# Second block's attention: two heads' values stationary on the halves of TensorE's array, exponentials divided before their turn, and no turn of the output

## The chip, the cores and the metric

The kernel runs on one NeuronCore of a Trainium2 chip, as one program in one launch. The metric is the device time of one execution in microseconds. Five engines run their own instruction streams in order and meet only at semaphores: TensorE (PE), which multiplies and turns (transposes), VectorE (DVE), ScalarE (ACT), GpSimd (POOL), and SyncE (SP), which here only starts the loads of the weights.

## The reference

Two transformer blocks in float32 on 256 tokens of width 1024. The first has differential attention, retention and a feed-forward part that picks among 16384 experts. The second has a state-space mixer (SSD, 16 heads of 64), a latent attention (MLA, 16 heads), a memory attention and a convolved feed-forward part. The change is in the latent attention of the second block, which for each of 16 heads computes

```python
scores = (q_h @ k_h.T) * 96 ** -0.5        # 256 x 256, q and k of width 96 (64 + 32 rotated)
p = softmax(where(causal by blocks of 64, scores, -inf))
out[:, h * 64:(h + 1) * 64] = p @ v_h      # values of width 64
```

The 1024 columns of `out` and the 1024 of the SSD mixer are then multiplied with a weight matrix of 2048 x 1024 and added to the residual stream.

## The kernel before

Tokens lie in two tiles of 128 (`t` = 0, 1). Most products are in a form that adds three products of rounded parts (a high and a low part of each operand), so weights stream in through SP, ACT rounds the high part of each slot (`hi_parts`, line L1580), POOL subtracts for the low part (L523), and PE multiplies. PE gives each slot back through the semaphore `spent`. The small products of attention are in plain float32. The trace shows each of those as two passes (a matmul of the program has two rows on PE), and a turn as one.

The attention of the second block and the convolution of the SSD mixer are written as one loop over the heads `h` = 0 to 15, once for each engine, with the order written out by hand. I call one turn of this loop an iteration. In iteration `h`

- PE makes the scores of head `h + 2` (`mla_scores`, L1241), turns the exponentials of head `h` into bank 5 (`mla_turn`, L1251), turns queries or keys (`qk_turn`, L1231), multiplies one slot of the SSD input, `xbc(7 + h)` up to `h` = 8 (L565, L566, L570), then `z_late` (L574, L575, L579) up to `h` = 12, then `out_half`, the first slots of the output matrix (same lines). In some iterations there are small products (`cb_product`, L1214; `cum`, L1203) and turns of the SSD input (`xs_turn`, L1222). Last comes `mla_out(h)` (L1261): exponentials times values.
- DVE masks the scores of `h + 2` and takes their maximum (`masked`, L2979, L2982), copies the turned exponentials of `h` to SBUF (L3044), convolves SSD channels (`conv(6 + h)`, L2901 to L2907, five instructions) and does the mask of `cb` (L2998, L2999) and `xs_out` (L3007, L3008).
- ACT copies turned queries and keys (`qk_out`, L2022, L2024), makes the exponentials of head `h + 2` and their sums (`mla_exp`, L2035), and rounds one weight slot (L1580). In iterations 2, 6 and 10 it applies Silu to four convolved tiles (`xbc_silu`, L1991), which takes a load of its function table, and one back for the exponential.

`xbc(pos)` writes one of two PSUM banks, so PE waits there until `conv(pos - 2)` is done: `if pos >= 4: pe.wait_ge(s["conv_done"], 4 * (pos - 1))`. In iteration `h` that is the convolution that DVE does in its iteration `h - 1`.

The output of head `h` comes out with tokens on the partitions, undivided, in bank 6, four heads at a time. Then DVE divides four heads by their sums (`divided`, L2989, L2990) into `o_m`, PE turns it (`out_turn`, L1271, in iterations 6 and 10 and after the loop), ACT makes the high part (`out_hi`, L2043) and DVE the low part (`out_lo`, L3014) of `m_t`, which `out_half` multiplies with the output matrix. After the loop comes the loop over the 16 SSD heads, in which PE waits for each head on a chain PE (`seg_sum`, L1277), DVE (`clip`, L3028), ACT (`seg_exp`, L2080, L2081), DVE (`weigh`, L3021), and does `out_half` in every second head.

Of the kernel before, what the change touches and what calls it, by code (L numbers as in the profile page):

```python
# [30 lines left out]
P = 128  # L31
# [167 lines left out]
OUT_AT = {6: (0, 3), 10: (1, 0)}  # L199
# [59 lines left out]
def _places(parts):  # L259
# [25 lines left out]
    kcat=(13312, 16384), seg=(14336, 16384), v_m=(16384, 18432), q_t=(18432, 22528), m_hi=(18432, 20480), m_lo=(20480, 22528),  # L285
    k_t=(22528, 26624), lat_hi=(22528, 23808), lat_lo=(23808, 25088), row_t=(25088, 25344), o_m=(27648, 29696), dts=(29696, 30208),
# [7 lines left out]
def two_blocks(nc, weights, consts, cols_in, rows_in, x_in, mem_in, pos_in, out):  # L294
    with ExitStack() as ctx:
# [61 lines left out]
        def row(name):  # L357
# [32 lines left out]
        o_m = area("o_m", "p (t c) -> p t c", t=TT)  # L390
# [28 lines left out]
            "cum_copied", "up_first", "xs_turned", "xdt_made", "o_turned", "group_factor", "mla_masked",  # L419
            "seg_sum", "seg_clipped", "seg_exp", "seg_weighed", "ssd_out",  # L420
            "group_root", "trig_arg", "trig_done", "kv_rotated",
            "mla_scores", "mla_shift", "mla_exp", "mla_turned", "mla_t_copied", "mla_out", "mla_out_copied",
# [130 lines left out]
        def _(pe):  # L553
# [691 lines left out]
            def mla_turn(h):  # L1245

                pe.wait_ge(s["mla_exp"], h + 1)
                if h:
                    pe.wait_ge(s["mla_t_copied"], h)
                for k in range(3):  # L1250
                    mm = pe.transpose(bank[:, 5, k * P:(k + 1) * P], e_m[:, h % 2, k * P:(k + 1) * P], ident)  # L1251
                mm.then_inc(s["mla_turned"], 1)

            def mla_out(h):

                pe.wait_ge(s["mla_t_copied"], h + 1)
                if h % 4 == 0 and h:
                    pe.wait_ge(s["mla_out_copied"], h // 4)
                for t in range(TT):
                    for k in range(t + 1):  # L1260
                        mm = pe.matmul(bank[:, 6, t * T + h % 4 * 64:t * T + h % 4 * 64 + 64], et_m[:, h % 2, t + k, :],  # L1261
                                       v_m[:, k, h * 64:(h + 1) * 64], start=(k == 0), stop=(k == t))
                mm.then_inc(s["mla_out"], 1)

            def out_turn(pair, to):

                pe.wait_ge(s["mla_out_copied"], pair + 1)
                for b in (2 * pair, 2 * pair + 1):
                    for t in range(TT):
                        at = (b % 2) * T + t * P  # L1270
                        mm = pe.transpose(bank[:, to, at:at + P], o_m[:, t, b * P:(b + 1) * P], ident)  # L1271
                mm.then_inc(s["o_turned"], 1)
# [38 lines left out]
            for h in range(MH):  # L1311
# [46 lines left out]
                mla_out(h)  # L1358
# [3 lines left out]
            out_turn(2, 7)  # L1362
            out_half(0, 1, m_t)
            done = AHEAD
            for h in range(SH):
# [8 lines left out]
                if h == 0:  # L1374
                    pe.wait_ge(s["mla_out_copied"], 4)
                if h == 4:
# [10 lines left out]
                if h == 0:  # L1387
                    low("mla_out", 5)
                    out_turn(3, 7)
# [176 lines left out]
        def _(act):  # L1566
# [473 lines left out]
            def out_hi(pair, at):  # L2040
                act.wait_ge(s["o_turned"], pair + 1)
                for b in (2 * pair, 2 * pair + 1):
                    nc.scalar.copy(m_t[0][:, b, :], bank[:, at, (b % 2) * T:(b % 2 + 1) * T]).then_inc(s["split_act"], 1)  # L2043
# [11 lines left out]
            hi_parts(M + 3)  # L2055
            for h in range(MH):
                for i in QK_AT.get(h, ())[:1]:
                    qk_out(i, 7)
                if h + 2 < MH:
# [3 lines left out]
                if h == 10:  # L2063
                    out_hi(*OUT_AT[h])
# [4 lines left out]
                if h == 6:  # L2069
                    out_hi(*OUT_AT[h])  # L2070
# [14 lines left out]
            out_hi(2, 7)  # L2085
# [13 lines left out]
            for h in range(SH):  # L2099
                if h:  # L2100
                    seg_exp(h)
                if h == 2:
                    out_hi(3, 7)
# [164 lines left out]
        def _(dve):  # L2268
# [717 lines left out]
            def divided(i):  # L2986
# [353 lines left out]
```

## Time and profile before

| what | value |
|---|---|
| median of 3 runs | 1451.14 us (1450.7 to 1451.85) |
| profiled execution, time | 1453.91 us |
| profiled execution, span on the core | 1452.1 us |
| PE busy | 1434.8 us, 99% of the span |
| DVE, ACT, POOL busy | 949.9, 825.6, 890.9 us |
| the chain that ended last | PE 90% |
| granted clock of TensorE, mean | 0.999 |
| the loop over the 16 heads, from PE's first scores in it to the first SSD head | 1060.7 to 1142.3 us of the span |

The span is what the profiler saw on the core; the time is that of the same execution by the device's clock and is 1.8 us longer. The profiled execution took 2.8 us more than the median.

### The profile page before, as it was taken

What the parts mean: (1) busy time and instruction counts of PE and PEld (TensorE: products, weight loads), DVE (VectorE), ACT (ScalarE), POOL (GpSimd) and SP (SyncE); (2) the same over time, 40 slices, a digit from 0 to 9 for tenths busy, and PEclk for the clock granted to TensorE, in tenths of its full rate; (3) what the DMA queues carried; (4) which work ended last, traced back from release to release, by engine and by line L of the source; (5) the groups of instructions that cost most, each with busy time, mean ns of one, the idle gap of its engine ahead of it and who ended that gap; (6) DMA issues with size and microseconds to landing.
All of it is one profiled execution on the core that took longest, in us unless ns stands there. A gap on an engine that the chain in (4) does not pass through costs nothing.

```text
span 1452.1 us, 25628 instructions
## 1 busy us (share of the span) xinstructions
PE 1434.8 (99%) x8868; PEld 1284.9 (88%) x8868; DVE 949.9 (65%) x2022; ACT 825.6 (57%) x1481; POOL 890.9 (61%) x711
## 2 busy tenths in 40 slices
PE   8999999999999999999999999999999999999997
PEld 6788999999999999888888888888899889888886
DVE  4664399948889999665555555334687633387776
ACT  6576555456666665554454554447666766644454
POOL 6749898987777777200000003997944576599986
PEclk9999999999999999999999999999999999999999
DMA  7535667655555555555555555655643454466664
GB/s 255 161 102 182 180 189 233 196 181 151 162 157 159 161 165 162 183 193 197 189 194 198 188 195 191 190 182 183 194 129 91 160 153 138 136 190 193 191 189 130
DMA packets 137590, 253.09 MB, mean 174 GB/s; under 512 B 16464, under 2 KB 18896, under 8 KB 136848
## 3 DMA queue, kind: packets, MB, share of 16 engines
q1 hardware_dynamic: 135392, 243.79, 53.7%
q10 hardware_dynamic: 1872, 6.41, 1.3%
q8 instruction: 63, 1.03, 0.3%
q0 software_dynamic: 224, 1.54, 0.3%
q14 instruction: 39, 0.32, 0.1%
HBM read 248.54 MB, written 3.15 MB: 173 GB/s over the span
## 4 chain that ended last, share of the span: by engine, by line
PE 90%; POOL 4%; DVE 2%; issue 2%; ACT 2%; DMA 1%; SPq 0%; POOLq 0%; ACTq 0%; DVEq 0%
PE bank L556 13%; PE bank L558 13%; PE bank L557 13%; PE bank L574 5%; PE bank L579 5%; PE bank L1517 5%; PE bank L575 5%; PE bank L570 5%; PE bank L565 5%; PE bank L566 5%; POOL w_both L523 3%; PE bank L1520 3%; PE bank L1002 2%; PE bank L1029 2%; PE bank L1032 1%
## 5 line engine op out<-in xcount | busy, mean ns | idle before, releaser
L523 POOL TENSOR_TENSOR w_both<-ring,w_both 128x512 fp32r<-128x512 f32 x688 | 873.4, 1299 | 546.2 <-ACT w_both L1580 537.7
L1580 ACT CAST w_both<-ring 128x1024 fp32r<-128x1024 f32 x452 | 474.7, 1051 | 378.8 <-PE bank L558 176.3
L2773 DVE TENSOR_TENSOR w_both<-ring,w_both 128x1024 fp32r<-128x1024 f32 x111 | 136.0, 1225 | 124.6 <-ACT w_both L1580 123.3
L556 PE MATMUL bank<-w_both,act_hi 128*128 128x512 f32 x512 | 199.5, 390 | 0.4 <-DVE act_lo L2778 0.4
L557 PE MATMUL bank<-w_both,act_hi 128*128 128x512 f32 x512 | 199.4, 389 | 0.0
L558 PE MATMUL bank<-w_both,act_lo 128*128 128x512 f32 x512 | 199.2, 389 | 0.0
L557 PE MATMUL bank<-h_both,w_both 128*128 128x256 f32 x648 | 183.4, 283 | 0.0
L556 PE MATMUL bank<-h_both,w_both 128*128 128x256 f32 x648 | 183.3, 283 | 0.0
L558 PE MATMUL bank<-h_both,w_both 128*128 128x256 f32 x648 | 183.3, 283 | 0.0
L565 PE MATMUL bank<-h_both,w_both 128*128 128x256 f32 x568 | 141.6, 287 | 0.0
L566 PE MATMUL bank<-h_both,w_both 128*128 128x256 f32 x568 | 139.2, 283 | 0.0
L556 PEld LDWEIGHTS bank<-h_both,w_both 128*128 128x128 f32 x648 | 124.4, 192 | 0.0
L558 PEld LDWEIGHTS bank<-h_both,w_both 128*128 128x128 f32 x648 | 124.4, 192 | 0.0
L557 PEld LDWEIGHTS bank<-h_both,w_both 128*128 128x128 f32 x648 | 124.3, 192 | 0.0
L556 PEld LDWEIGHTS bank<-w_both,act_hi 128*128 128x128 f32 x512 | 96.2, 188 | 20.5 <-DVE w_both L2773 0.8
L558 PEld LDWEIGHTS bank<-w_both,act_lo 128*128 128x128 f32 x512 | 96.1, 188 | 20.1
L557 PEld LDWEIGHTS bank<-w_both,act_hi 128*128 128x128 f32 x512 | 96.2, 188 | 19.4
L566 PEld LDWEIGHTS bank<-h_both,w_both 128*128 128x128 f32 x568 | 108.9, 192 | 0.2
L565 PEld LDWEIGHTS bank<-h_both,w_both 128*128 128x128 f32 x568 | 108.8, 191 | 0.2
L2726 DVE TENSOR_TENSOR hots<-bank,chosen_t 128x1024 fp32r<-128x1024 f32 x64 | 78.4, 1224 | 10.1 <-PE bank L1002 6.0
L570 PE MATMUL bank<-h_both,w_both 128*128 128x256 f32 x600 | 83.9, 283 | 0.0
L574 PE MATMUL bank<-w_both,h_both 128*128 128x512 f32 (+2 forms) x208 | 81.8, 395 | 0.4 <-issue 0.3
(482 smaller groups left out, 2711.0 us busy)
## 6 DMA issues: line engine op xcount, KB each, us to landing
ring<-weights_in SPq DMA_DIRECT2D x910, 256.0 KB, 3.0
mem_kv<-arena ACTq DMA_DIRECT2D x2, 1024.0 KB, 6.9
arena<-mem_kv ACTq DMA_DIRECT2D x2, 1024.0 KB, 8.4
ring<-weights_in SPq DMA_DIRECT2D x8, 200.0 KB, 2.6
ring<-weights_in SPq DMA_DIRECT2D x8, 144.0 KB, 2.4
xres<-x_in SPq DMA_DIRECT2D x2, 512.0 KB, 5.3
arena<-mem_in POOLq DMA_DIRECT2D x1, 1024.0 KB, 8.5
arena<-rows_in ACTq DMA_DIRECT2D x2, 512.0 KB, 4.1
```

The lines of the kernel that those rows point to most:

```text
L523: nc.gpsimd.tensor_tensor(w_lo[:, k, at], ring[:, k, at], w_hi[:, k, at].bitcast(F32), ALU.subtract).then_inc(s[done], 1)
L556: pe.matmul(out_, a[0], b[0], start=start, stop=False, **kw)
L557: pe.matmul(out_, a[0], b[1], start=False, stop=False, **kw)
L558: return pe.matmul(out_, a[1], b[0], start=False, stop=stop, **kw)
L565: pe.matmul(out_, w[0], b[0], start=start, stop=False, skip_group_check=True)
L566: return pe.matmul(out_, w[0], b[1], start=False, stop=False, skip_group_check=True)
L570: return pe.matmul(out_, w[1], b[0], start=False, stop=stop, skip_group_check=True)
L574: pe.matmul(out_, x[0], w[0], start=start, stop=False, skip_group_check=True)
L575: return pe.matmul(out_, x[1], w[0], start=False, stop=False, skip_group_check=True)
L1580: nc.scalar.copy(w_hi[:, k, :], ring[:, k, :]).then_inc(s["hi_made"], 1)
L2726: link(v.tensor_tensor(hots, iota8, chosen_t[:, 0:2, 4 * g:4 * g + 4].unsqueeze(3).broadcast_to([P, 2, 4, NK]), ALU.is_equal))
L2773: v.tensor_tensor(w_lo[:, k, :], ring[:, k, :], w_hi[:, k, :].bitcast(F32), ALU.subtract)\
```

## The change

`mla_out` takes two heads at once, at the end of odd iterations only. The values of a head (128 keys by 64) are now the stationary operand and lie in one half of the array's columns, the two heads in the two halves; the turned exponentials are the moving operand, 256 tokens for the first 128 keys and 128 tokens for the second. The output has channels on the partitions and tokens along the row, which is what `m_t` needs, so `o_m`, `divided` and `out_turn` are gone. Since the tokens are then no longer on the partitions, the exponentials are divided before they are turned: DVE takes the reciprocal of the sums of one head (`inverse`), and ACT scales the exponentials in place (`e_scaled`). PE's turn waits for that instead of for the exponential. `out_hi` and `out_lo` take 256 columns of bank 6 after each pair of heads, in even iterations, and `mla_out` of the next pair waits for `out_lo`. `m_lo` moves to where `o_m` was.

```diff
             def mla_turn(h):
-                pe.wait_ge(s["mla_exp"], h + 1)
+                pe.wait_ge(s["mla_scaled"], h + 1)
...
-            def mla_out(h):
-
-                pe.wait_ge(s["mla_t_copied"], h + 1)
-                if h % 4 == 0 and h:
-                    pe.wait_ge(s["mla_out_copied"], h // 4)
-                for t in range(TT):
-                    for k in range(t + 1):
-                        mm = pe.matmul(bank[:, 6, t * T + h % 4 * 64:t * T + h % 4 * 64 + 64], et_m[:, h % 2, t + k, :],
-                                       v_m[:, k, h * 64:(h + 1) * 64], start=(k == 0), stop=(k == t))
+            def mla_out(pair):
+
+                pe.wait_ge(s["mla_t_copied"], 2 * pair + 2)
+                if pair:
+                    low("mla_out", pair - 1)
+                for k in range(TT):
+                    for e in range(2):
+                        h = 2 * pair + e
+                        mm = pe.matmul(bank[64 * e:64 * e + 64, 6, k * P:T], v_m[:, k, h * 64:(h + 1) * 64],
+                                       et_m[:, e, 2 * k:2 + k, :].rearrange("p k q -> p (k q)"), start=(k == 0), stop=(k == 1),
+                                       skip_group_check=True)
                 mm.then_inc(s["mla_out"], 1)
-
-            def out_turn(pair, to):
...
-                if h == 10:
-                    pe.wait_ge(s["conv_done"], 60)
-                    out_turn(1, 0)
...
-                    out_turn(0, 3)
...
-                mla_out(h)
+                if h % 2:
+                    mla_out(h // 2)
...
+            def e_scaled(h):
+                act.wait_ge(s["mla_inverse"], h + 1)
+                for t in range(TT):
+                    e = e_m[:, h % 2, t * P:t * P + (t + 1) * P]
+                    ins = nc.scalar.mul(e, e, dts[:, 256 + t * MH + h:257 + t * MH + h])
+                ins.then_inc(s["mla_scaled"], 1)
+
+            def out_hi(pair):
+                act.wait_ge(s["mla_out"], pair + 1)
+                nc.scalar.copy(m_t[0][:, pair, :], bank[:, 6, 0:T]).then_inc(s["split_act"], 1)
...
             hi_parts(M + 3)
+            e_scaled(0)
             for h in range(MH):
                 for i in QK_AT.get(h, ())[:1]:
                     qk_out(i, 7)
+                if h + 1 < MH:
+                    e_scaled(h + 1)
                 if h + 2 < MH:
                     mla_exp(h + 2)
                 if h in (2, 6, 10):
                     xbc_silu(h + 2)
-                if h == 10:
-                    out_hi(*OUT_AT[h])
+                if h % 2 == 0 and h:
+                    out_hi(h // 2 - 1)
                 if 3 + h < 16:
                     hi_parts(M + 4 + h)
...
+            def inverse(h):
+                dve.wait_ge(s["mla_exp"], h + 1)
+                v.reciprocal(m_div[:, :, h:h + 1], m_sum[:, :, h:h + 1]).then_inc(s["mla_inverse"], 1)
...
+            def out_lo(pair):
+                dve.wait_ge(s["split_act"], SPLIT["mla_out"] + pair + 1)
+                v.tensor_tensor(m_t[1][:, pair, :], bank[:, 6, 0:T], m_t[0][:, pair, :].bitcast(F32), ALU.subtract).then_inc(s["lo_made"], 1)
...
             for h in range(MH):
+                if h + 1 < MH:
+                    inverse(h + 1)
                 if h + 2 < MH:
                     masked(h + 2)
-                if h % 4 == 0 and h:
-                    divided(h // 4 - 1)
                 dve.wait_ge(s["mla_turned"], h + 1)
                 if h >= 2:
-                    dve.wait_ge(s["mla_out"], h - 1)
+                    dve.wait_ge(s["mla_out"], h // 2)
                 v.tensor_copy(et_m[:, h % 2, :, :], bank[:, 5, 0:3 * P].rearrange("p (k q) -> p k q", q=P))\
                     .then_inc(s["mla_t_copied"], 1)
-                if h - 1 in OUT_AT:
-                    out_lo(*OUT_AT[h - 1])
+                if h % 2 == 0 and h:
+                    out_lo(h // 2 - 1)
                 if 6 + h < 16:
                     conv(6 + h)
```

After the loop `out_hi(7)` stands behind `seg_exp(0)` on ACT and `out_lo(7)` between `weigh(0)` and `clip(1)` on DVE, where `out_hi(2)`, `divided(3)` and `out_lo(2)` stood. `out_turn(2)` and `out_turn(3)` with their parts are gone.

**ACT, iteration 6 of the loop.** In the kernel before these are the exponentials of head 8 (L2035), the table load and the four Silu (L1991), the weight slot (L1580), and the two high parts of the turned output (L2043):

```order
L2024 ACTIVATE arena<-bank 96x512 [waits qk_turned]
L2022 COPY arena<-bank 96x512 [waits qk_turned]
L2035 ACTIVATE work,arena<-bank,arena 128x128 [waits mla_turned,mla_shift]
L2035 ACTIVATE work,arena<-bank,arena 128x256
L1991 ACT_TABLE_LOAD
L1991 ACTIVATE arena<-arena 128x256 [waits conv_done] x4
L1580 CAST w_both<-ring 128x1024 [waits spent,slot_loaded_1]
L2043 CAST m_hi<-bank 128x256 [waits o_turned]
L2043 CAST m_hi<-bank 128x256
```

In the changed kernel L2026 is `e_scaled(7)`, L2017 the exponentials of head 8, L1973 Silu, L2031 `out_hi(2)` and L1562 the weight slot:

```order
L2006 ACTIVATE arena<-bank 96x512 [waits qk_turned]
L2004 COPY arena<-bank 96x512 [waits qk_turned]
L2026 ACTIVATE work<-work,arena 128x128 [waits mla_inverse]
L2026 ACTIVATE work<-work,arena 128x256
L2017 ACTIVATE work,arena<-bank,arena 128x128 [waits mla_turned,mla_shift]
L2017 ACTIVATE work,arena<-bank,arena 128x256
L1973 ACT_TABLE_LOAD
L1973 ACTIVATE arena<-arena 128x256 [waits conv_done] x4
L2031 CAST m_hi<-bank 128x256 [waits mla_out]
L1562 CAST w_both<-ring 128x1024 [waits spent,slot_loaded_1]
```

Two scalings came in ahead of the exponentials, and the high part moved from behind the weight slot to right behind the Silu. Iteration 2 has the same order now and had no high part before.

**DVE, iteration 6 of the loop, and on to iteration 7.** Before, the copy of the turned exponentials (L3044) was followed by `conv(12)` and then by the masking of the next iteration:

```order
L2982 TENSOR_REDUCE arena<-bank 128x1
L3044 COPY work<-bank 128x384 [waits mla_out,mla_turned]
L2901 TENSOR_TENSOR bank<-bank,arena 128x256 [waits spent]
L2903 TENSOR_SCALAR arena<-bank,cols 128x256 [waits xbc_scaled]
L2907 SCALAR_TENSOR_TENSOR arena<-bank,cols,arena 128x255 [waits conv_done]
L2907 SCALAR_TENSOR_TENSOR arena<-bank,cols,arena 128x254 [waits conv_done]
L2907 SCALAR_TENSOR_TENSOR arena<-bank,cols,arena 128x253 [waits conv_done]
L2979 TENSOR_TENSOR bank<-bank,arena 128x2x128 [waits mla_exp,mla_scores]
```

Now L3025 is the copy, L2995 `out_lo(2)`, which waits through `split_act` for `out_hi(2)`, and L2888 the first instruction of `conv(12)`; L2975 is `inverse(8)`:

```order
L2969 TENSOR_REDUCE arena<-bank 128x1
L3025 COPY work<-bank 128x384 [waits mla_out,mla_turned]
L2995 TENSOR_TENSOR m_lo<-bank,m_hi 128x256 [waits split_act]
L2888 TENSOR_TENSOR bank<-bank,arena 128x256 [waits spent]
L2890 TENSOR_SCALAR arena<-bank,cols 128x256 [waits xbc_scaled]
L2894 SCALAR_TENSOR_TENSOR arena<-bank,cols,arena 128x255 [waits conv_done]
L2894 SCALAR_TENSOR_TENSOR arena<-bank,cols,arena 128x254 [waits conv_done]
L2894 SCALAR_TENSOR_TENSOR arena<-bank,cols,arena 128x253 [waits conv_done]
L2975 RECIPROCAL arena<-arena 128x2 [waits mla_exp]
```

The low part of a pair of heads came in between the copy and the convolution, in every even iteration from 2 on.

**PE, end of iteration 5.** Before, the last rows of the iteration and the first of the next (L1214 is `cb_product`, L1261 `mla_out(5)`, L1241 the scores of head 8, L1251 the turn of head 6):

```order
L1214 MATMUL bank<-arena 128x256
L1261 MATMUL bank<-arena,work 128x64 [waits mla_t_copied]
L1261 MATMUL bank<-arena,work 128x64 x2
L1241 MATMUL bank<-arena 128x128 [waits mla_exp,qk_out_act]
L1241 MATMUL bank<-arena 128x256
L1251 MATMUL bank<-cst,work 128x128 [waits mla_t_copied,mla_exp]
```

Now (L1212, L1260 for heads 4 and 5, L1239, L1249):

```order
L1212 MATMUL bank<-arena 128x256
L1260 MATMUL bank<-work,arena 64x256 [waits lo_made,mla_t_copied]
L1260 MATMUL bank<-work,arena 64x256
L1260 MATMUL bank<-work,arena 64x128 x2
L1239 MATMUL bank<-arena 128x128 [waits mla_exp,qk_out_act]
L1239 MATMUL bank<-arena 128x256
L1249 MATMUL bank<-cst,work 128x128 [waits mla_t_copied,mla_scaled]
```

Three narrow products per head became four wider ones per pair of heads, each on 64 output partitions, with a wait for the low part of the pair before, and the turn waits for the scaled exponentials.

## Rows read from the trace of the kernel before

**Rows 1.** The page, busy time, share of the span, instructions.
```profile
PE 1434.8 (99%) x8868; PEld 1284.9 (88%) x8868; DVE 949.9 (65%) x2022; ACT 825.6 (57%) x1481; POOL 890.9 (61%) x711
```

**Rows 2.** Groups by line, 1050 to 1190 us: busy us, mean ns.
```profile
L1261 PE MATMUL bank<-arena,work 128*128 128x64 f32 x96 | 12.5, 267 | 0.0
...
L3014 DVE TENSOR_TENSOR m_lo<-bank,m_hi 128x256 fp32r<-128x256 f32 x8 | 3.0, 417 | 0.0
...
L2122 ACT ACTIVATE arena<-arena 128x256 f32<-128x256 f32 x4 | 1.7, 498 | 0.3 <-DVE arena L3102 0.3
...
L2989 DVE RECIPROCAL arena<-arena 128x8 f32<-128x8 f32 x4 | 0.8, 195 | 0.0
```

**Rows 3.** Timeline of PE in and behind the loop: start us, length us.
```profile
1061.39 0.49 PE L1251 MATMUL bank<-cst,work 128*128 128x128 f32 x3
...
1073.04 0.87 PE L1241 MATMUL bank<-arena 96*128 96x128 f32 x4
...
1080.27 0.36 PE L565 MATMUL bank<-h_both,w_both 128*128 128x256 f32 x1
...
1096.81 0.87 PE L1241 MATMUL bank<-arena 96*128 96x128 f32 x4
...
1101.16 0.60 PE L1271 MATMUL bank<-cst,arena 128*128 128x128 f32 x4
1101.59 0.78 PE L1261 MATMUL bank<-arena,work 128*128 128x64 f32 x6
1102.21 0.87 PE L1241 MATMUL bank<-arena 96*128 96x128 f32 x4
...
1103.61 0.36 PE L565 MATMUL bank<-h_both,w_both 128*128 128x256 f32 x1
...
1115.03 0.50 PE L574 MATMUL bank<-w_both,h_both 128*128 128x512 f32 x1
...
1123.64 0.63 PE L1222 MATMUL bank<-cst,arena 128*128 128x128 f32 x4
```

**Rows 4.** Timeline of ACT, before the loop and in iteration 6.
```profile
1060.99 1.05 ACT L1580 CAST w_both<-ring 128x1024 fp32r<-128x1024 f32 x1 [0.48 <-PE bank L570]
...
1098.49 0.58 ACT L2022 COPY arena<-bank 96x512 f32<-96x512 f32 x1 [1.80 <-PE bank L1231]
1098.97 0.36 ACT L2035 ACTIVATE work<-bank,arena 128x128 f32<-128x128 f32 x1
...
1099.90 1.28 ACT L1991 ACT_TABLE_LOAD   x1
1101.19 1.34 ACT L1991 ACTIVATE arena<-arena 128x256 f32<-128x256 f32 x4
1102.43 1.03 ACT L1580 CAST w_both<-ring 128x1024 fp32r<-128x1024 f32 x1
```

**Rows 5.** Timeline of DVE in iterations 6 and 8.
```profile
1099.19 0.42 DVE L2901 TENSOR_TENSOR bank<-bank,arena 128x256 f32<-128x256 f32 x1
...
1100.23 1.52 DVE L2907 SCALAR_TENSOR_TENSOR arena<-bank,cols,arena 128x255 f32<-128x255 f32 x3
...
1114.29 0.68 DVE L3008 TENSOR_TENSOR arena<-bank,arena 128x512 f32<-128x512 f32 x1
```

**Rows 6.** Timeline of PE: products on row halves, and on the whole array.
```profile
90.77 1.13 PE L847 MATMUL bank<-arena 64*128 64x256 f32 x8
91.84 0.50 PE L574 MATMUL bank<-w_both,h_both 128*128 128x512 f32 x1
...
1089.06 1.03 PE L1214 MATMUL bank<-arena 128*128 128x256 f32 x4
1089.93 0.78 PE L1261 MATMUL bank<-arena,work 128*128 128x64 f32 x6
```

**Rows 7.** Stretches at the end: us, PE busy (x), granted clock, DMA share, GB/s.
```profile
1446.00:1448.00 2.00, 0.00 (x0) 1.00 0.00 0
1448.00:1450.00 2.00, 0.00 (x0) 0.69 0.87 312
```

More of the change, by code:

```diff
@@ L418, in two_blocks @@
             "xbc_silu", "latent_summed", "rotated", "y_ready", "y_summed", "y_scaled", "y_scaled_late", "qk_turned", "qk_out_act",
[L419 removed]
+            "cum_copied", "up_first", "xs_turned", "xdt_made", "group_factor", "mla_masked",
             "seg_sum", "seg_clipped", "seg_exp", "seg_weighed", "ssd_out",
             "group_root", "trig_arg", "trig_done", "kv_rotated",
[L422 removed]
+            "mla_scores", "mla_shift", "mla_exp", "mla_turned", "mla_t_copied", "mla_out", "mla_inverse", "mla_scaled",
             "mem_scores", "mem_shift", "mem_exp", "mem_scaled", "mem_turned", "mem_t_copied", "mem_out", "mem_out_copied",
@@ L1386, in _ @@
                           start=False, stop=True).then_inc(s["ssd_out"], 1)
-                if h == 0:
-                    low("mla_out", 5)
-                    out_turn(3, 7)
             while done < 2 * KD:
@@ L2038, in mla_exp @@
                 ins.then_inc(s["mla_exp"], 1)
[L2040 to L2043, printed above, removed]
+            def e_scaled(h):
[7 more added lines that the diff above has]
+                nc.scalar.copy(m_t[0][:, pair, :], bank[:, 6, 0:T]).then_inc(s["split_act"], 1)
             act.dma_start(area("mask"), consts[:, CAT["mask"][0]:CAT["mask"][1]]).then_inc(s["mask_loaded"], 16)
@@ L2084, in _ @@
             seg_exp(0)
-            out_hi(2, 7)
+            out_hi(7)
             def y_squares(g):
@@ L2984, in masked @@
                 ins.then_inc(s["mla_shift"], 1)
-            def divided(i):
-                dve.wait_ge(s["mla_out"], 4 * i + 4)
-                hs = slice(4 * i, 4 * i + 4)
-                link(v.reciprocal(m_div[:, :, hs], m_sum[:, :, hs]))
-                v.tensor_tensor(o_m[:, :, i * T:(i + 1) * T].rearrange("p t (h c) -> p t h c", c=64),
-                                bank[:, 6, :].rearrange("p (t h c) -> p t h c", t=TT, c=64),
-                                m_div[:, :, hs].unsqueeze(3).broadcast_to([P, TT, 4, 64]), ALU.mult)\
-                    .then_inc(s["mla_out_copied"], 1)
+            def inverse(h):
+                dve.wait_ge(s["mla_exp"], h + 1)
+                v.reciprocal(m_div[:, :, h:h + 1], m_sum[:, :, h:h + 1]).then_inc(s["mla_inverse"], 1)
             def cb_mask(g):
@@ L3009, in xs_out @@
                     .then_inc(s["xdt_made"], 1)
-            def out_lo(pair, at):
-                dve.wait_ge(s["split_act"], SPLIT["mla_out"] + 2 * pair + 2)
-                for b in (2 * pair, 2 * pair + 1):
-                    v.tensor_tensor(m_t[1][:, b, :], bank[:, at, (b % 2) * T:(b % 2 + 1) * T], m_t[0][:, b, :].bitcast(F32), ALU.subtract)\
-                        .then_inc(s["lo_made"], 1)
+            def out_lo(pair):
+                dve.wait_ge(s["split_act"], SPLIT["mla_out"] + pair + 1)
+                v.tensor_tensor(m_t[1][:, pair, :], bank[:, 6, 0:T], m_t[0][:, pair, :].bitcast(F32), ALU.subtract).then_inc(s["lo_made"], 1)
             def weigh(h):
@@ L3033, in _ @@
             masked(1)
+            inverse(0)
             conv(5)
@@ L3079, in _ @@
             weigh(0)
-            divided(3)
+            out_lo(7)
             clip(1)
-            out_lo(2, 7)
             dve.wait_ge(s["copied_act"], COPY["z_late"][0] + 2)
@@ L3088, in _ @@
                 weigh(h + 1)
-                if h == 2:
-                    out_lo(3, 7)
                 if h in (4, 8, 12):
```

19 lines of the change are left out of this document (2 added, 17 removed).

## The prediction

> **What bounds the kernel now.** I read the page first: PE is busy for 1434.8 us of the span of 1452.1, DVE for 65% of it [rows 1]. So PE's own work is the time, and a change is worth what it takes off PE less what it makes PE wait. Then I read the timelines of PE, ACT and DVE over the loop, to see how close behind PE the others are. I name times by their distance from an iteration's start on PE. In iteration 6 (start 1096.81) PE reaches the next slot of the SSD input, `xbc(14)`, at 1103.61, that is at 6.8 [rows 3]. It needs `conv(12)` there, whose five instructions DVE runs from 1099.19 to 1101.75 (1100.23 + 1.52), so they end at 4.95 [rows 5]. The slack is 1.85 us. It is the number on which this prediction turns.
>
> **Work taken off PE.** `mla_out` of a head holds PE for 0.62 us (1101.59 to 1102.21 [rows 3]; 96 passes in all, six per head [rows 2]). Sixteen of them make 9.8 us. A turn of the output holds it for 0.43 (1101.16 to 1101.59 [rows 3]) with four transposes; the other three stand in a denser place, so I take 0.37 for them, and 1.5 for all four.
>
> **Work put on PE.** Each pair has four products, that is eight passes: four over 256 columns, four over 128. On the whole array four passes over 256 columns take 0.87 us (1089.06 to 1089.93), 0.215 each. One after the other the pair would take 4 x 0.215 + 4 x 0.108 = 1.29 us. No row shows column halves, but the retention's products on row halves alternate in the same way: eight passes over 256 columns from 90.77 to 91.84, 1.07 us where the whole array would need 1.72 [rows 6]. That is just five lengths: a product's second pass runs beside the first pass of the product on the other half, and only the first and the last are alone. The same count for the new pair gives 1 + 1 + 0.5 + 0.5 + 0.5 + 0.5 = 4 lengths, 0.86 us. Going to halves and back costs something, since the first weight loads cannot be early; the bounds are 0.86 and 1.07 (the row itself), and I take 0.95. Eight pairs make 7.6 us. Net of work: 7.6 - 9.8 - 1.5 = -3.7 us.
>
> The Trainium skill speaks against this price. "TensorEngine Tiling (Array Packing)", Key Properties, says that a change of tiling mode drains the engine; a row that shows the drain alone is not there, and by that rule the pair would be nearer 1.07. "TensorE: Matmul & The Clock Gate", Part 3 (The mechanism), says that a weight load overlaps with a running product only when the row groups differ, and two column halves share all rows. By that rule little of the overlap is left; it is the rival of no overlap below.
>
> **The wait at the start.** On ACT `e_scaled(0)` stands behind a weight slot that runs from 1060.99 to 1062.04 [rows 4], because the slot's place comes free only when PE has finished the slot before the loop. PE turned head 0 at 1061.39 [rows 3]. The price of two scalings in place (128 and 256 columns) has no row. Nearest is a scaling of 256 columns in place, 0.50 us [rows 2]; below it lies the 0.36 of an exponential of 128 [rows 4]. For the two, pipelined, the bounds are 0.65 and 1.0; I take 0.75. So PE turns head 0 at 1062.75: a wait of 1.35 us.
>
> **The waits in iterations 3 and 7.** Take iteration 6. ACT copies the turned queries at 1.68 and starts the exponentials at 2.16, the table load at 3.09, Silu at 4.38 to 5.72 [rows 4]. Now `e_scaled(7)` comes before the exponentials: Silu ends at 6.45. Behind it stands `out_hi(2)`, about 0.35 us: 6.8. On DVE `out_lo(2)` stands between the copy and `conv(12)` and waits for that, then takes 0.42 [rows 2]: 7.2. What is queued behind it is the whole convolution, 2.56 us: it ends at 9.8 instead of 4.95. PE comes to `xbc(14)` at 6.8 less the turn of 0.43 and the `mla_out` of 0.62 that left iteration 6, so at 5.75. It waits **4.0 us**. Iteration 2 has the same chain. There PE came to `xbc(10)` at 80.27 - 73.04 = 7.2 [rows 3], now 0.6 earlier, 6.6, and `conv(8)` ends at 9.7: a wait of **3.0 us**. In iterations 4, 8 and 12 there is no Silu, so `out_hi` ends at 4.2 and the convolution at 7.1, which PE meets with hardly a wait. In iteration 8, however, the convolution is followed by `xs_out(1)`, whose end at 1114.97 [rows 5] lies right ahead of the part of `z_late` that needs its bank, at 1115.03 [rows 3]: no slack. `out_lo(3)` with its wait and the reciprocal put it 1.0 us later on balance (the division of four heads is gone from DVE), and PE comes 0.6 us earlier: 1.6 us.
>
> **The wait in iteration 11.** PE's `xs_turn` at 1123.64 [rows 3] already follows the last Silu of iteration 10. That Silu starts with the scores of iteration 10 and not with PE's later work, so the `mla_out` and the turn that left iteration 10 (1.0 us) only bring PE there earlier, and DVE's reciprocal adds 0.15: 1.15 us more. Behind the loop `e_scaled(15)`, two high parts and a low part stand ahead of the first SSD heads on ACT and DVE, while a turn is gone from PE: an estimate of 0.8 us with what is left over in iterations 5 and 13, between 0 and 1.5.
>
> **The sum.** Waits 1.35 + 3.0 + 4.0 + 1.6 + 1.15 + 0.8 = 11.9 us, work -3.7: +8.2 us. The rest is free: the scalings of the other heads lie in idle time of ACT (it waits 1.80 us in iteration 6 [rows 4]), the weight slots are rounded three slots ahead, and the division that leaves DVE was hidden. Nothing later gives the loss back, because PE is the bound on both sides of the loop. The profiled execution would go from 1453.9 to 1462.1; on the median, 2.8 lower, 1451.1 becomes **1459.4 us**.
>
> **Rivals.**
> 1. *The work counts and the convolution does not wait.* Then -3.7 is nearly all: 1447.4. For it: ACT and DVE are far from full [rows 1]. Against it: both rows of order are hard, and a load of ACT's table and Silu (2.6 us) lie between. It decides at waits of 3.7 us in all; the one of iteration 7 alone passes that. With about half of my waits the result is no change.
> 2. *The column halves do not overlap.* The pair takes 1.29 plus 0.1; eight cost 3.5 us more, a little of it inside waits: 1462.5. For it: no row has column halves. Against it: the row halves count out to five lengths exactly.
> 3. *The clock falls in a wait.* Behind the last matmul the granted clock still is 1.00 from 1446 to 1448 with PE idle, and 0.69 in the next stretch [rows 7], so it fell from 2.4 to 1.2 GHz near 1448.8, when PE had been idle for more than 2.8 us. Waits of 3.0 and 4.0 us are in that region. Work from 1096.81 to 1101.16 [rows 3], 4.35 us, would take twice that at the lower level; with one fall, part of it hidden by the next wait, 3 us more: 1462.5.
>
> **How the numbers follow.** My forecast 0.6, rival 2 0.14, rival 3 0.12, rival 1 0.06, half the waits (near no change) 0.08. The forecast's own range: scalings -0.3 to +0.8, pairs -0.7 to +1.0, the last term -0.8 to +0.7, so 1457.6 to 1461.9. Rivals 2 and 3 with their errors reach to 1466; below, 1454.5 leaves rival 1 and no change outside. Within 0.2% (2.9 us) is what a measurement of this kernel can't tell from no change. Faster 0.06, same 0.08, slower 0.86.
>
> **What the new profile would show.** Two waits of PE on DVE's convolution, 3.0 us before `xbc(10)` and 4.0 before `xbc(14)`; ahead of each, DVE idle with ACT's high part as the releaser. A wait of 1.35 us of PE on ACT's scaling at the loop's start. Eight groups of eight passes of about 0.95 us each, instead of sixteen of 0.62. The loop up to the first SSD head 8 us longer than the 81.6 before, with the same time on both sides of it. I am wrong if the low part finds its high part ready in iterations 2 and 6, or if a group takes 1.3 us, or if the clock is below 1.00 in the loop.

## The result, and the profile after

The changed kernel takes 1462.38 us (median of 6 runs, 1461.15 to 1462.74), the kernel before 1451.22 (6 runs, 1450.62 to 1452.54). The ratio is 1.0073, with a 95% interval of 1.0063 to 1.0083: 11 us slower, where 8.2 were predicted. The time lies 3.0 us above the forecast. That is 0.5 us outside the forecast's own range (1457.6 to 1461.9), but inside the wider one (1454.5 to 1466) that counts rivals 2 and 3 in, and both of these had put it at 1462.5. So the time alone doesn't tell which of them came; the rows and the experiments do.

The page of the changed kernel, busy time, share of the span and instructions, answers to [rows 1]:

```profile
PE 1433.8 (98%) x8820; PEld 1279.0 (88%) x8820; DVE 945.7 (65%) x2030; ACT 836.7 (57%) x1513; POOL 892.2 (61%) x711
```

PE is busy for 1.0 us less and the span is 1460.5 us, 8.4 more: on balance the loss is idle time of PE. (The busy time holds the slow stretches shown below, so it fell by less than the work did.) The view of waits of PE on others, from 1040 to 1200 us (us in total, times, longest), names the places; in the kernel before it has one row there, of 0.2 us and ahead of the loop:

```profile
PE bank L563 <- DVE arena L2894: 6.6, 2, 3.7
PE bank L572 <- DVE arena L2990: 1.3, 1, 1.3
PE bank L1249 <- ACT work L2026: 1.2, 1, 1.2
PE bank L1220 <- ACT arena L1973: 0.9, 1, 0.9
PE bank L1268 <- DVE arena L3001: 0.4, 1, 0.4
```

L563 is `xbc`, which waits for the convolution (L2894); L572 `z_late`, which waits for `xs_out` (L2990); L1249 the turn of head 0 behind its scaling (L2026); L1220 `xs_turn` behind Silu (L1973); L1268 the sums of an SSD head. These are the places of the forecast. The releasers can be followed in the timelines (start us, length us, in brackets the idle time before and who ended it). PE, answering to [rows 3]:

```profile
1078.22 0.60 PE L1229 MATMUL bank<-cst,arena 128*96 128x128 f32 x4
1081.67 0.38 PE L563 MATMUL bank<-h_both,w_both 128*128 128x256 f32 x1 [2.85 <-DVE arena L2894]
...
1086.00 0.74 PE L1229 MATMUL bank<-cst,arena 128*96 128x128 f32 x4
...
1105.08 0.60 PE L1229 MATMUL bank<-cst,arena 128*96 128x128 f32 x4
1109.39 0.39 PE L563 MATMUL bank<-h_both,w_both 128*128 128x256 f32 x1 [3.71 <-DVE arena L2894]
...
1113.85 0.60 PE L1220 MATMUL bank<-cst,arena 128*128 128x128 f32 x4
```

ACT in iteration 6, answering to [rows 4]:

```profile
1101.90 0.81 ACT L2026 ACTIVATE work<-work,arena 128x128 f32<-128x128 f32 x2
...
1103.52 1.28 ACT L1973 ACT_TABLE_LOAD   x1
1104.82 1.33 ACT L1973 ACTIVATE arena<-arena 128x256 f32<-128x256 f32 x4
1106.06 0.35 ACT L2031 CAST m_hi<-bank 128x256 fp32r<-128x256 f32 x1
```

DVE in iteration 6, answering to [rows 5]:

```profile
1101.66 0.55 DVE L3025 COPY work<-bank 128x384 f32<-128x384 f32 x1
1106.44 0.42 DVE L2995 TENSOR_TENSOR m_lo<-bank,m_hi 128x256 fp32r<-128x256 f32 x1 [4.23 <-ACT m_hi L2031]
1106.78 0.42 DVE L2888 TENSOR_TENSOR bank<-bank,arena 128x256 f32<-128x256 f32 x1
...
1107.82 1.51 DVE L2894 SCALAR_TENSOR_TENSOR arena<-bank,cols,arena 128x255 f32<-128x255 f32 x3
```

This is the predicted chain: DVE stands still for 4.23 us at the low part of a pair of heads until ACT, behind the table load and four Silu, has made the high part; the convolution queued behind it ends at 1109.3, and PE begins `xbc(14)` at 1109.39. It could have begun at 1105.44 (a turn takes 0.36 before the next slot starts, as everywhere in the loop), so the wait is 3.95 us. In iteration 2 the same rows stand at 1078.72 to 1081.6, and `xbc(10)` starts 3.1 us late. (The idle time in brackets is smaller, because it is counted from the modelled end of the last matmul.)

The groups by line, from 1050 to 1190 us (busy us, mean ns of one, idle time before), answer to [rows 2]:

```profile
L2026 ACT ACTIVATE work<-work,arena 128x256 f32<-128x256 f32 x16 | 7.9, 496 | 0.0
L2026 ACT ACTIVATE work<-work,arena 128x128 f32<-128x128 f32 x16 | 6.4, 401 | 7.4 <-DVE arena L2975 7.4
L1260 PE MATMUL bank<-work,arena 128*64 128x256 f32 x32 | 5.2, 404 | 0.0
...
L2995 DVE TENSOR_TENSOR m_lo<-bank,m_hi 128x256 fp32r<-128x256 f32 x8 | 3.4, 422 | 15.8 <-ACT m_hi L2031 15.8
L1260 PE MATMUL bank<-work,arena 128*64 128x128 f32 x32 | 3.1, 273 | 0.0
```

The eight low parts take 3.4 us and wait 15.8 for their high parts. Most of that does not reach PE; the two waits of 4.23 us do.

The stretches of 2 us around the two waits (PE busy and its instructions, granted clock, share of the DMA engines, GB/s) answer to [rows 7] and show what the forecast left out of its sum:

```profile
1078.00:1080.00 2.00, 0.82 (x8) 1.00 0.00 0
1080.00:1082.00 2.00, 0.33 (x2) 1.00 0.01 3
1082.00:1084.00 2.00, 2.00 (x15) 0.72 0.70 220
1084.00:1086.00 2.00, 2.00 (x11) 0.50 0.11 39
1086.00:1088.00 2.00, 2.00 (x16) 0.93 0.00 0
1106.00:1108.00 2.00, 0.00 (x0) 1.00 0.00 0
1108.00:1110.00 2.00, 0.61 (x5) 1.00 0.10 12
1110.00:1112.00 2.00, 2.00 (x13) 0.55 0.68 239
1112.00:1114.00 2.00, 2.00 (x13) 0.60 0.03 11
1114.00:1116.00 2.00, 2.00 (x18) 1.00 0.00 0
```

Behind each of the two waits the clock fell to its lower level, 1.2 GHz. The slot `xbc(10)` takes 4.33 us (1081.67 to 1086.00) and `xbc(14)` 4.46 (1109.39 to 1113.85), where a slot of the same form at 1.00 takes 2.95 (1073.42 to 1076.37): 1.4 and 1.5 us more. The turn behind `xbc(10)` takes 0.68 us where it takes 0.53 at 1.00, another 0.15. These are the costs in this one execution; in other profiled executions with the same waits a fall costs up to 2.8 us (see the kernels `heads_in_turn` and `first_scaling_early`).

The loop from the first scores to the first SSD head takes 91.5 us instead of 81.6, that is +9.9. What is behind it takes 0.5 more. Ahead of the loop, where both kernels run the same program, the profiled execution of the kernel before was 2.1 us longer than that of the changed one. Its first scores for the loop start at 1056.54, in the changed kernel at 1054.45, and in the ten experiments below between 1053.4 and 1055.2, so it is the profile of before that stands apart. Of the 2.1 us, 0.7 is in waits of PE for rounded weights and other parts from 990 us on (0.9 against 0.2); the rest isn't attributed. That accounts for most of why the profiles differ by 8.4 us and the medians by 11.2; some 0.7 us between the two stays open.

### The profile page after: what moved, and what is told of

The parts are those of the page before. It is cut to its first block, busy times and chain, and to the rows that moved or that the text cites. A ratio compares the mean times of both kernels' runs of the same rounds, so it can differ in the third digit from the quotient of the medians.

```text
span 1460.5 us, 25572 instructions
## 1 busy us (share of the span) xinstructions
PE 1433.8 (98%) x8820; PEld 1279.0 (88%) x8820; DVE 945.7 (65%) x2030; ACT 836.7 (57%) x1513; POOL 892.2 (61%) x711
## 4 chain that ended last, share of the span: by engine, by line
PE 88%; DVE 4%; ACT 3%; POOL 2%; issue 2%; DMA 1%; SPq 0%; ACTq 0%; POOLq 0%; DVEq 0%
PE bank L554 13%; PE bank L556 13%; PE bank L555 13%; PE bank L1499 5%; PE bank L568 5%; PE bank L577 5%; PE bank L572 5%; PE bank L573 5%; PE bank L563 5%; PE bank L564 5%; PE bank L1502 3%; PE bank L1000 2%; POOL w_both L521 2%; PE bank L1027 2%; PE bank L1030 1%
## 5 line engine op out<-in xcount | busy, mean ns | idle before, releaser
L1562 ACT CAST w_both<-ring 128x1024 fp32r<-128x1024 f32 x452 | 474.2, 1050 | 375.3 <-PE bank L556 175.4
L563 PE MATMUL bank<-h_both,w_both 128*128 128x256 f32 x568 | 142.9, 289 | 6.6 <-DVE arena L2894 6.6
L563 PEld LDWEIGHTS bank<-h_both,w_both 128*128 128x128 f32 x568 | 109.7, 193 | 7.3 <-DVE arena L2894 7.1
L572 PE MATMUL bank<-w_both,h_both 128*128 128x512 f32 (+2 forms) x208 | 81.8, 395 | 1.7 <-DVE arena L2990 1.3
```

The lines of the kernel that those rows point to most:

```text
L563: pe.matmul(out_, w[0], b[0], start=start, stop=False, skip_group_check=True)
L572: pe.matmul(out_, x[0], w[0], start=start, stop=False, skip_group_check=True)
L1562: nc.scalar.copy(w_hi[:, k, :], ring[:, k, :]).then_inc(s["hi_made"], 1)
```

## The experiments

Each kernel is the changed one with the edit shown. Times are medians; the kernel before, measured beside each, is given with it. The last four add up edits.

**VectorE's low part behind the convolution** (`low_after_conv`). It tells whether the order on DVE makes the two long waits.

```diff
-                if h % 2 == 0 and h:
-                    out_lo(h // 2 - 1)
                 if 6 + h < 16:
                     conv(6 + h)
+                if h % 2 == 0 and h:
+                    out_lo(h // 2 - 1)
```

> The changed kernel with one edit: on DVE the low part of a pair stands behind the convolution of its iteration instead of ahead of it. Theory (the order makes the convolution late): the waits of PE before xbc(10) and xbc(14), 3.1 and 3.95 us, vanish, and with them the two stretches at the lower clock (2.9 us); the wait of iteration 9 stays at 1.5 to 1.8 us, since the low part still stands ahead of xs_out. Time 1452.5 us. Rival (the added scalings and reciprocals load ACT and DVE, wherever they stand): the waits shrink little and the time stays above 1459. Rival (the products on column halves are dear): no change, 1462.

Measured: 1452.81 us against 1452.27, ratio 1.0002 (0.9992 to 1.0011). PE's wait for L2894 is gone, the mean clock goes from 0.997 to 0.998, and 0.0071 of the time, 10.3 us, is back. The two waits (7.05 us) and the two falls of the clock (2.9 us) come to 9.95. One place in an order carries nearly the whole loss.

**ScalarE's high part ahead of the table load and Silu** (`high_before_silu`). The same chain, cut at its other end: DVE's order stays.

```diff
-                if h in (2, 6, 10):
-                    xbc_silu(h + 2)
                 if h % 2 == 0 and h:
                     out_hi(h // 2 - 1)
+                if h in (2, 6, 10):
+                    xbc_silu(h + 2)
```

> The changed kernel with one edit: on ACT the high part of a pair stands ahead of the table load and the four Silu of iterations 2, 6 and 10 instead of behind them. Theory: the high part ends 4.2 us behind the iteration's start and the convolution 7.1 behind it, so PE waits 0.5 us before xbc(10) and 1.4 before xbc(14) in place of 3.1 and 3.95; the clock stays at full level. Time 1454.5 us. Rival (load of ACT and DVE, not order): above 1459.

Measured: 1454.81 us against 1452.27, ratio 1.0018 (1.0009 to 1.0028). Two waits for the convolution stay (0.20 and 1.06 us of idle time, before `xbc(10)` and `xbc(14)`), since the low part still waits for the high part, which ACT makes behind scalings and exponentials. The mean clock is 0.999.

**PE kept at work in the two long waits** (`filler`). It takes the clock's fall out of the loss and leaves the waits: 15 and 23 products whose result nothing reads, in iterations 3 and 7, ahead of the slot that has to wait.

```diff
+                if h in (3, 7):
+                    pe.wait_ge(s["mla_exp"], h + 2)
+                    for i in range(15 if h == 3 else 23):
+                        pe.matmul(bank[:, 4, T:2 * T], h_t[0][:, 0, 0:P], h_t[0][:, 0, 0:T], start=True, stop=True, skip_group_check=True)
```

> The changed kernel with idle time filled: in iterations 3 and 7 PE runs 15 and 23 more products (128x256 of rounded parts, 0.12 us each, result unused) in front of the slot that it waits for. They fit into the waits of 3.1 and 3.95 us, so nothing starts later. Theory (the clock fell because PE was idle for so long, and that cost 2.9 us by itself): the granted clock stays at 1.00 through the loop and the time is 1459.5 us. Rival (the fall has another cause, or the slow stretches would have been waited for anyway): 1462.4 us.

Measured: 1460.04 us against 1452.27, ratio 1.0054 (1.0038 to 1.0071). The stretches around the second wait, of this kernel, in the same columns:

```profile
1106.00:1108.00 2.00, 1.41 (x12) 1.00 0.00 0
1108.00:1110.00 2.00, 1.63 (x13) 1.00 0.43 125
1110.00:1112.00 2.00, 2.00 (x19) 1.00 0.48 137
```

The clock stays at 1.00, and the first slot takes 2.98 us (1082.12 to 1085.10) instead of 4.33. The convolution still comes as late as it did. The gain is 0.0019 of the time, 2.8 us, between the ratios' medians; the intervals of the two overlap, so its size rests on the rows more than on the times. Against the next kernel, which was measured beside this one and has the changed kernel's waits, it is 2.4 us (1462.45). PE is not busy all through: 1.07 us of idle time stay ahead of `xbc(10)`, and no fall follows.

**The products of a pair, head by head** (`heads_in_turn`). The forecast counted "five lengths" for a group on halves, because a product's second pass was taken to run beside the first pass of the next product, in the program's order. With the order changed so that both products of one head come first, that count gives more.

```diff
-                for k in range(TT):
-                    for e in range(2):
+                for e in range(2):
+                    for k in range(TT):
```

> The changed kernel with the four products of a pair in the order head, then keys, so that both products of one head stand together instead of alternating between the column halves. Theory (passes run in order, and only passes on different halves overlap): 5.5 lengths of a pass over 256 columns instead of 4, the group goes from 0.80 to about 1.12 us, eight groups give 2.6 us: 1465.0 us. Rival (the halves do not overlap, the passes are cheap for another reason): group and time as in the changed kernel, 0.80 and 1462.4.

Measured: 1462.45 us against 1452.27, ratio 1.0068 (1.0051 to 1.0085), and a group of 0.81 us. The order makes no difference, so the count by order fell.

The profiled execution of this kernel (1463.88 us, above its median) shows something else. The clock falls here while PE is still idle, and the slot starts at the lower level. The stretches up to `xbc(14)`, which starts at 1109.65:

```profile
1107.65:1108.65 1.00, 0.00 (x0) 1.00 0.00 0
1108.65:1109.65 1.00, 0.00 (x0) 0.64 0.00 0
```

The slot then takes 5.29 us instead of 4.46, and the turn behind it 0.93 instead of 0.53: this fall costs 2.7 us, with the same wait ahead of it (3.71 us of idle time in both).

**Both heads on the same half of the columns** (`same_half`). The second head's product goes to other columns of the bank, which nothing reads, so the output leaves out the odd heads.

```diff
-                        mm = pe.matmul(bank[64 * e:64 * e + 64, 6, k * P:T], v_m[:, k, h * 64:(h + 1) * 64],
+                        mm = pe.matmul(bank[0:64, 6, e * T + k * P:(e + 1) * T], v_m[:, k, h * 64:(h + 1) * 64],
```

> The changed kernel with both heads of a pair on the same half of the array's columns, in two places of the PSUM bank; the output of the second head of each pair is then not used, and output is wrong in those channels. Theory (the two halves run abreast, each with its own stream, in whatever order the products stand): here the eight passes run one after the other, 4 x 0.215 + 4 x 0.108 = 1.29 us and about 0.15 for the start and end, the group goes from 0.80 to about 1.4 us and the time up by 8 x 0.6 = 4.8 us: ratio to before 1.011. Rival (64 columns of weights make a pass cheap by themselves): 0.80 and no change.

Measured: 1467.63 us against 1452.21, ratio 1.0105 (1.009 to 1.0121), and a group of 1.44 us. The time holds more of the clock's fall than the changed kernel's profile does (the slot `xbc(14)` takes 5.29 us here), so the comparison rests on the groups. They stand so in the timelines of PE: the changed kernel, with the instruction behind it,

```profile
1071.18 0.87 PE L1260 MATMUL bank<-work,arena 128*64 128x256 f32 x8
1071.98 0.92 PE L1239 MATMUL bank<-arena 96*128 96x128 f32 x4
```

and the kernel with one half:

```profile
1071.58 1.51 PE L1260 MATMUL bank<-work,arena 128*64 128x256 f32 x8
1073.02 0.92 PE L1239 MATMUL bank<-arena 96*128 96x128 f32 x4
```

How many passes run at once can be read from stretches of L1260 alone, some 0.2 us long (the count in brackets is of the passes under way in the stretch). With one half of the columns:

```profile
1071.50:1071.75 0.25, 0.17 (x1) 1.00 0.00 0
1071.75:1072.00 0.25, 0.25 (x2) 1.00 0.00 0
```

With both halves, head by head (a pass begun in one stretch still counts in the next):

```profile
1071.55:1071.80 0.25, 0.17 (x2) 1.00 0.00 0
1071.80:1072.00 0.20, 0.20 (x4) 1.00 0.00 0
```

On one half a second pass joins only after the first stretch; on two halves two are there from the beginning, though in the program three more passes of head 0 stand ahead of the first of head 1. So the two halves work off their products independently. The trace does not name the head of a record; that the second is of the other head follows from the kernel with one half, where it isn't there.

**The first scaling ahead of the weight slot** (`first_scaling_early`).

```diff
+            e_scaled(0)
             hi_parts(M + 3)
-            e_scaled(0)
```

> The changed kernel with one edit: on ACT the scaling of head 0 stands ahead of the weight slot before the loop instead of behind it. Theory (the wait at the loop's start comes from that slot, which can begin only when PE has finished the slot before the loop): the wait of 1.4 us goes and nothing else changes, 1461.0 us. Rival (the scaling itself is late because the reciprocal is): 1462.4.

Measured: 1461.62 us against 1452.21, ratio 1.0065 (1.005 to 1.008). The wait at L1249 is gone from PE's waits; the gain of 0.0008, 1.2 us, is inside the intervals. In the profiled execution the clock falls during both long waits again, and `xbc(14)` takes 5.28 us.

**Both orders mended** (`both_moves`): the first scaling early, and the low part at the end of DVE's iteration.

```diff
+            e_scaled(0)
             hi_parts(M + 3)
-            e_scaled(0)
...
-                if h % 2 == 0 and h:
-                    out_lo(h // 2 - 1)
                 if 6 + h < 16:
                     conv(6 + h)
...
+                if h % 2 == 0 and h:
+                    out_lo(h // 2 - 1)
```

> The changed kernel with the first scaling ahead of the weight slot and the low part of a pair at the end of its DVE iteration, behind the convolution and xs_out. Theory: the waits at the start (1.4 us), of the convolution (7.0), of iteration 9 (1.3) and the clock's 2.9 us go; 1.3 us stay in iteration 11 and at the first SSD heads. Ratio to before 0.9988 (1.7 us faster). Rival (each removed wait comes back at the next place): not faster than before.

Measured: 1451.54 us against 1452.21, ratio 0.9994 (0.9985 to 1.0004). PE's waits from 1050 to 1200 us:

```profile
PE bank L1220 <- ACT arena L1973: 1.2, 1, 1.2
PE bank L572 <- DVE arena L2990: 0.7, 1, 0.7
PE bank L1268 <- DVE arena L3001: 0.4, 1, 0.4
PE bank L1229 <- ACT arena L2006: 0.4, 1, 0.4
```

**Four moves** (`four_moves`): besides, in iteration 10 ACT's Silu goes ahead of the exponentials, and the last low part behind `clip(1)`.

```diff
+                if h == 10:
+                    xbc_silu(h + 2)
                 if h + 2 < MH:
                     mla_exp(h + 2)
-                if h in (2, 6, 10):
+                if h in (2, 6):
                     xbc_silu(h + 2)
...
-            out_lo(7)
             clip(1)
+            out_lo(7)
```

> The kernel both_moves with two more moves: in iteration 10 the Silu stands ahead of the exponentials on ACT, and behind the loop the last low part stands behind the second clip on DVE. Theory: the waits of iteration 11 (0.9 us) and of the first SSD heads (0.4) go as well; ratio to before 0.998 (3.0 us faster), which is the work that left PE less what its switches cost. Rival (the table load for the exponential now comes late for the heads 12 and 13): as both_moves or slower.

Measured: 1450.9 us against 1452.21, ratio 0.9991 (0.9982 to 1.0). The waits at L1220 and L1268 are gone, and a new one came: PE waits 1.0 us at `mla_out(5)` for the copy of turned exponentials. The timeline of DVE shows what made that copy late:

```profile
1122.56 0.43 DVE L2997 TENSOR_TENSOR m_lo<-bank,m_hi 128x256 fp32r<-128x256 f32 x1 [4.55 <-ACT m_hi L2031]
...
1123.96 0.55 DVE L3027 COPY work<-bank 128x384 f32<-128x384 f32 x1
```

The low part waits for its high part in `both_moves` too, 3.42 us. With the Silu brought forward, the table load back and the exponentials stand ahead of the high part as well, so it comes 1.0 us later (1122.16 instead of 1121.14), and so does the copy behind the low part.

**The high part first on ScalarE, with two moves and with four** (`high_first`, `five_moves`). The edit of both:

```diff
+                if h % 2 == 0 and h:
+                    out_hi(h // 2 - 1)
                 if h + 1 < MH:
                     e_scaled(h + 1)
...
-                if h % 2 == 0 and h:
-                    out_hi(h // 2 - 1)
```

> The version with both moves (first scaling early, VectorE's low half of the output at the end of its iteration), and in the even iterations of ScalarE the rounded high half of the output comes first, ahead of the scaling of exponentials. Theory (what is left of the loss is in single waits of the even iterations, and ScalarE's order sets them): the low half never waits for the high half; the wait of 0.7 us for the low half (L572) and that of 0.4 us for the scaling shrink by together some 0.6 us or the second grows to 0.8, the waits of 1.2 us at the Silu (L1220) and 0.4 us at the first SSD head stay. Ratio to before about 0.999 (1450.8 us), against 0.9994 of the version without the move. Rival: the scaling, now 0.35 us later, is late for its values product in every even iteration, and the ratio rises to 1.001.

> The version with four moves, and the high half of the output first on ScalarE in the even iterations. Theory: in iteration 10 the low half's wait of 4.55 us for the high half goes, and with it the 1.0 us that TensorE waited for the copy of the fifth pair's sums (L1260 on L3027); ratio to before about 0.998 (1449.3 us) where the version with four moves has 0.9991. Rival: the wait comes back at the next place in the row, as it did with four moves, and the ratio stays at 0.999.

Measured: with two moves 1449.82 us, ratio 0.9987 (0.9978 to 0.9996); with four 1449.5 us, ratio 0.9986 (0.9977 to 0.9995), against 1451.73. The waits of PE in the same stretch, with two moves,

```profile
PE bank L1220 <- ACT arena L1973: 1.0, 1, 1.0
PE bank L1268 <- DVE arena L3001: 0.8, 2, 0.4
PE bank L1229 <- ACT arena L2006: 0.4, 1, 0.4
```

and with four:

```profile
PE bank L1260 <- DVE work L3027: 0.4, 1, 0.4
PE bank L1229 <- ACT arena L2006: 0.4, 1, 0.4
PE bank L1268 <- DVE arena L3003: 0.3, 1, 0.3
```

The last one waits 1.1 us in all, so its work of -4.1 us (below) should leave -3.0; measured are -2.0 (-3.3 to -0.7). The intervals of the two hardly differ, so which of them is the faster is open. With four moves the wait at L1260 shrank from 1.0 to 0.4 us and did not go, so the forecast of 0.998 did not quite come. Both lie below the kernel before with intervals clear of 1, by 0.13% and 0.14%, which is less than the 0.2% that the prediction took as the least a measurement can tell.

## Why the prediction was nearly right, point by point

**The work** was sized well. A group is 0.80 us from its start to the start of the scores behind it, and the scores then take 0.76 instead of 0.65: 0.91 for a group in all, forecast 0.95. Eight make 7.3. Sixteen products of 0.62 are 9.9 (the prediction wrote 9.8), so 7.3 - 9.9 - 1.5 = -4.1 us instead of -3.7. Two more differences cancel: the row ahead of a group is some 0.09 us longer (L1212 holds PE for 0.96 instead of 0.87), and each old `mla_out` had made the scores behind it 0.06 longer (0.71 instead of 0.65); each comes to about 0.8 us over the loop.

The step that gave that size was wrong in its mechanism: "That is just five lengths: a product's second pass runs beside the first pass of the product on the other half, and only the first and the last are alone." The runs show two independent halves instead. Four passes of one head, two over 256 columns and two over 128, are 2 x 0.215 + 2 x 0.108 = 0.65 us; the group's 0.91 less that leaves 0.26, and with the 0.09 ahead of it 0.35, for going to halves and back and for the weights. The row halves of [rows 6] read so too: four passes of 0.215 are 0.86, and 1.07 holds 0.21 besides. The rule "second pass beside first pass" would have misjudged a pair in another order by 0.3 us a group (the kernel with heads in turn).

The Trainium skill, "TensorEngine Tiling (Array Packing)", Key Properties, says that different tiles can load weights and multiply in parallel; the 0.80 us of two halves against 1.44 of one agree. Its other rule there, the drain at a change of mode, has no row of its own; the 0.35 us bound it from above. The Trainium skill, "TensorE: Matmul & The Clock Gate", Part 3 (The mechanism), says that a weight load overlaps with a running product only when the row groups differ. The prediction drew from it that column halves would hardly overlap. That does not hold for these groups: 0.80 us on two halves, 1.44 on one. So rival 2 (1.29 us and 0.1 for a pair) fell.

**The waits** came where the forecast put them, and nearly as long:

| place | forecast, us | measured, us |
|---|---|---|
| turn of head 0 | 1.35 | 1.4 |
| `xbc(10)`, iteration 3 | 3.0 | 3.1 |
| `xbc(14)`, iteration 7 | 4.0 | 3.95 |
| `z_late`, iteration 9 | 1.6 | 1.5 |
| `xs_turn`, iteration 11 | 1.15 | 0.9 |
| behind the loop and elsewhere | 0.8 | 0.9 |
| sum | 11.9 | 11.75 |

The two scalings are 0.80 us, taken at 0.75. Of the last row, 0.5 us is the difference behind the loop, and 0.4 the turn (0.37) that is gone from there. Rival 1, work without a wait, gave 1447.4; no kernel reached it: the lowest, five edits away, has 1449.5 with 1.1 us of waits left, beside a kernel before of 1451.73.

**The term that was missing** is rival 3, the fall of the clock. The forecast wrote: "The clock falls in a wait" and gave it a chance of 0.12 and a price of 3 us. It came, twice, at 1.4 and 1.5 us in the profiled execution (1.5 each with the slowed turn). The prediction's own sign of being wrong, "if the clock is below 1.00 in the loop", came with it. The kernel with filler shows the cause: with PE at work through most of the same waits the clock keeps 1.00. The step that failed is the choice of the likeliest case, and the evidence against it was in the prediction's own text: "when PE had been idle for more than 2.8 us. Waits of 3.0 and 4.0 us are in that region." The fall belonged in the sum: 1459.4 + 2.9 = 1462.3, with 1462.38 measured. That this meets the median so closely is in part luck. The terms as measured (waits 11.75, clock 2.9, work -4.1) make 10.55 us, where the medians are 11.2 apart; dearer falls in the executions that weren't profiled could fill the gap, which isn't shown. For the price of a fall varies: 1.3 to 1.5 us behind the first wait, and 1.5, 2.3, 2.7 and 2.8 behind the second, in the four profiled executions that have these waits. The forecast's price was given as one fall of 3 us; it was two of about half that here, because the clock rose again around the end of the slot (1.00 from 1114 on).

**The sum by the profile of after**: in the loop, waits 10.85, clock 2.9, work 7.3 - 9.9 and three turns of together 1.2, that is 9.95, where the loop is 9.9 longer. The forecast's "with the same time on both sides of it" held behind the loop (0.5) and not ahead of it, where the profiled execution of before ran 2.1 us longer in the same program. So an agreement of profiles alone would have hidden the missing term: the profiled time forecast was 1462.1 and came out as 1462.28, for two errors that cancel.

## What to carry to other kernels

Where an engine takes over a step with a wait in the middle of an in-order row, price everything behind that step, not the step: here 0.42 us of subtraction cost 10 us, because the convolution stood behind it; behind it PE's waits for the convolution were gone, though the low part still waited for its high part (7.8 us in four waits, in `low_after_conv`). When a forecast contains a wait of PE as long as one behind which the trace shows the clock to fall, put the fall in the sum. And compare profiles by stage, first of all in a stage that the change leaves alone.

## What the runs showed that was not expected

- How soon the clock falls, and for how long, differs between executions with the same waits. In the changed kernel's profile it reads 1.00 through both waits (1106 to 1108, PE busy 0.00) and falls when work is back: the records of `xbc(10)` stand 0.12 us apart up to 1082.84, 1.2 us behind its start, and 0.215 apart from 1083.23 on. In `heads_in_turn` and `first_scaling_early` it falls with PE still idle in both waits, in `same_half` in the second, and in the kernel before with PE idle at the end [rows 7]. So it isn't the return of work that brings the fall. The waits of 1.5 us and less in the same loop had no fall behind them; between 1.5 and 3.1 us nothing was tried.
- Column halves run two plain float32 products, each of two passes, fully abreast, and the order in which the program gives the products does not matter (0.80 and 0.81 us a group; 1.44 on one half).
- Removing a wait by moving a step brought a wait at the next place three times (1.0 us at L1260 in the kernel with four moves, 0.4 at L1229 in five kernels, 1.2 at L1220 where 0.9 was). The one move of the low part gave back 10.3 us; all later moves together added only some 2.3 (0.0016 of the time).
